# Eight column sums of a modulation product: reduced after a transpose, or by one-column matmuls

## The reference: what is computed

```python
def modulation(cond, ada_w, ada_b):
    mod = jax.nn.silu(cond) @ ada_w + ada_b            # ada_w: 2048 x 18432
    return jnp.split(mod[..., None, :], N_MOD, axis=-1)
...
sh1, sc1, g1, sh2, sc2, g2, sh3, sc3, g3 = modulation(c, ada_w[l], ada_b[l])
xs = ffn_sublayer(xs, sh1, sc1, g1, norm_ffn1_w[l], ffn1_wi[l], ffn1_wo[l])
mq, mk, mv, mo, mg, aq, ak, av, gm, ga = mixer_inputs(xs, sh2, sc2, norm_mix_w[l], w_in[l])
hm, _ = mlstm_branch(...)                              # 4 heads, two directions
ha = latent_attention(...)                             # 16 query heads, 4 key heads
xs = xs + g2 * merge_branches(hm, ha, gm, ga, w_proj_m[l], w_proj_a[l], w_out[l])
xs = ffn_sublayer(xs, sh3, sc3, g3, norm_ffn2_w[l], ffn2_wi[l], ffn2_wo[l])
```

## Time and profile before

| | |
|---|---|
| median of three runs | 2280.02 us |
| the profiled execution's own time | 2280.02 us |
| its span, first to last instruction | 2278.2 us |
| TensorE matmul busy | 2234.8 us (98%) in 10699 matmuls |
| VectorE busy | 1525.6 us (67%) |
| ScalarE busy | 934.5 us (41%) |
| TensorE's share of the chain that ended last | 93% |
| granted TensorE clock | 0.998 |

### The profile page before, as it was taken

How to read it: one execution, slowest core, us unless ns; L and a number is a source line. 1 busy time by engine, 2 the same in 40 slices (tenths; PEclk the granted TensorE clock), 3 DMA queues, 4 the chain that set the end, 5 groups by cost and what they waited for, 6 DMA issues and landing times.

```text
span 2278.2 us, 28667 instructions
## 1 busy us (share of the span) xinstructions
PE 2234.8 (98%) x10699; PEld 1773.9 (78%) x10699; DVE 1525.6 (67%) x1746; ACT 934.5 (41%) x1096; POOL 63.0 (3%) x54
## 2 busy tenths in 40 slices
PE   6999999999999998999999999999999999999998
PEld 3567777777777777888878888888888888888887
DVE  3445766677667768854866888656567676776757
ACT  3333333333333335544554444445444443444442
POOL 0010000000000000000500000100000000000000
PEclk9999999999999999999999999999999999999999
DMA  9998878878887875553635777646576757657563
GB/s 362 377 377 298 298 280 284 287 269 303 278 293 257 312 278 185 193 184 123 212 117 190 257 256 252 207 165 197 191 259 193 263 189 249 196 195 261 185 225 125
DMA packets 273216, 548.08 MB, mean 241 GB/s; under 512 B 9022, under 2 KB 9222, under 8 KB 272896
## 3 DMA queue, kind: packets, MB, share of 16 engines
q1 hardware_dynamic: 212388, 421.59, 54.5%
q10 hardware_dynamic: 57740, 115.90, 14.3%
q0 software_dynamic: 3024, 9.71, 1.4%
HBM read 543.71 MB, written 3.46 MB: 240 GB/s over the span
## 4 chain that ended last, share of the span: by engine, by line
PE 93%; DVE 4%; DMA 2%; issue 1%; ACT 1%; SPq 0%; POOL 0%; ACTq 0%; DVEq 0%; POOLq 0%
PE ps L663 29%; PE ps L665 28%; PE ps L664 28%; PE ps L576 3%; DMA ada_w_sb<-in_ada_w 1%; DVE w_lo L1654 1%; PE ps L747 1%; DMA gate_bc<-gate_dram 1%; PE ps L617 0%; PE ps L589 0%; PE ps L598 0%; PE ps L650 0%; PE ps L609 0%; PE ps L991 0%; PE ps L1059 0%
## 5 line engine op out<-in xcount | busy, mean ns | idle before, releaser
L1654 DVE TENSOR_TENSOR w_lo<-raw_w,w_hi 128x1024 fp32r<-128x1024 f32 x728 | 896.9, 1234 | 570.2 <-ACT w_hi L1233 567.9
L1233 ACT CAST w_hi<-raw_w 128x1024 fp32r<-128x1024 f32 x728 | 764.6, 1052 | 1190.6 <-PE ps L665 1138.7
L663 PE MATMUL ps<-w_hi,xT_hi 128*128 128x512 f32 x2080 | 823.4, 396 | 6.7 <-DVE xT_lo L1734 4.0
L665 PE MATMUL ps<-w_hi,xT_lo 128*128 128x512 f32 x2080 | 810.8, 390 | 0.0
L664 PE MATMUL ps<-w_lo,xT_hi 128*128 128x512 f32 x2080 | 810.2, 390 | 0.0
L663 PEld LDWEIGHTS ps<-w_hi,xT_hi 128*128 128x128 f32 x2080 | 390.7, 188 | 114.2 <-issue 26.8
L665 PEld LDWEIGHTS ps<-w_hi,xT_lo 128*128 128x128 f32 x2080 | 390.7, 188 | 82.7
L664 PEld LDWEIGHTS ps<-w_lo,xT_hi 128*128 128x128 f32 x2080 | 391.1, 188 | 78.2
L663 PE MATMUL ps<-w_hi,hT_hi 128*128 128x512 f32 x704 | 277.8, 395 | 5.6 <-DVE hT_lo L1803 2.8
L665 PE MATMUL ps<-w_hi,hT_lo 128*128 128x512 f32 x704 | 274.7, 390 | 0.0
L664 PE MATMUL ps<-w_lo,hT_hi 128*128 128x512 f32 x704 | 274.5, 390 | 0.0
(11 more groups left out here) (276 smaller groups left out, 1017.7 us busy)
## 6 DMA issues: line engine op xcount, KB each, us to landing
raw_w<-in_ffn_wi SPq DMA_DIRECT2D x176, 1024.0 KB, 5.2
ada_w_sb<-in_ada_w ACTq DMA_DIRECT2D x96, 1024.0 KB, 7.5
raw_w<-in_ffn_wo SPq DMA_DIRECT2D x88, 1024.0 KB, 5.1
raw_w<-in_w_in SPq DMA_DIRECT2D x68, 1024.0 KB, 5.3
ada_w_sb<-in_ada_w SPq DMA_DIRECT2D x30, 1024.0 KB, 12.7
raw_w<-in_w_out SPq DMA_DIRECT2D x16, 1024.0 KB, 5.2
ada_m<-in_ada_w ACTq DMA_DIRECT2D x12, 1024.0 KB, 5.6
raw_w<-in_w_proj_m SPq DMA_DIRECT2D x8, 1024.0 KB, 5.1
```

Of the source, the lines that this page charges most:

```text
L663: pe.matmul(out, a_hi, w_hi[:, slot, kk, :], start=(first and kk == 0), stop=False)
L665: mm = pe.matmul(out, a_lo, w_hi[:, slot, kk, :], start=False, stop=(last and kk == 1))
L1233: act.copy(w_hi[:, us % SPL, :, :], raw_w[:, slot, 2 * half:2 * half + 2, :]).then_inc(hi_ready, 1)
L1654: dve.tensor_tensor(w_lo[:, us % SPL, :, :], raw_w[:, slot, 2 * half:2 * half + 2, :], w_hi[:, us % SPL, :, :].bitcast(F32), ALU.subtract) ...
```

## The change

`vec_T` becomes `column_sums`. Each of the eight 128x128 blocks of an accumulator is now the stationary operand of a float32 matmul whose moving operand is one column of ones. The sum over partitions comes out in one column of PSUM, 8 columns for each accumulator, all in bank 6. `sum_cols` loses the reduction and adds the bias straight from PSUM. In `U_OUT` the three accumulators are summed at one place, after unit 9, and one addition on VectorE takes all three. In `U_IN` the sum moves from after unit 27 to after unit 24, and its addition from VectorE's step 28 to step 26. `MACS_Z` spreads the 32 MACs evenly over steps 2 to 22, two in even and one in odd steps.

```diff
-MACS_Z = macs_at(*((v, 1 if v in (5, 9, 13) else 2) for v in range(2, 17)), (22, 2), (23, 2), (25, 1))
+MACS_Z = macs_at(*((v, 2 if v % 2 == 0 else 1) for v in range(2, 23)), (23, 0))
...
-            def vec_T(c, vec, done, bank):
+            def column_sums(c, accs, done):
 
                 pe.wait_ge(ada_cols_done, c)
                 pe.wait_ge(mac_done, done)
-                for g in range(GROUPS):
+                for n, vec in enumerate(accs):
                     for b in range(4):
-                        mm = pe.transpose(ps[:, bank + g, b * P:(b + 1) * P], vec[:, g, b * P:(b + 1) * P], ident)
-                mm.then_inc(acc_T_done, 1)
+                        for g in range(GROUPS):
+                            at = 8 * n + 2 * b + g
+                            mm = pe.matmul(ps[:, 6, at:at + 1], vec[:, g, b * P:(b + 1) * P], ctile[:, 0, 16:17], start=True, stop=True)
+                mm.then_inc(ada_summed, len(accs))
...
-                                vec_T(t + 4 * G3 - 1, vec_acc, t * VEC + VEC_F2, 6)
+                                column_sums(t + 4 * G3 - 1, [vec_acc], t * VEC + VEC_F2)
...
-                if v == 11:
-                    vec_T(VCH, vec_acc, VEC_M, 6)
+                if v == 8:
+                    column_sums(VCH, [vec_acc], VEC_M)
...
                     if n == 1 and k == 1:
-                        vec_T(VCH + 1, vec_m[0], VEC_F2, 4)
-                        vec_T(VCH + 1, vec_m[1], VEC_F2, 6)
-                    if n == 2 and k == 1:
-                        vec_T(VCH + 3, vec_m[2], VEC_F2, 4)
+                        column_sums(VCH + 1, vec_m, VEC_F2)
...
-            def sum_cols(c, bank):
-
-                n = c - VCH + 1
-                dve.wait_ge(ada_cols_done, c)
-                dve.wait_ge(acc_T_done, n)
-                dve.tensor_reduce(small[:, 48:56], ps[:, bank:bank + 2, :].rearrange("p g (b k) -> p (g b) k", k=P), AX.X, ALU.add
-                                  ).then_inc(acc_summed, 1)
-                dve.wait_ge(acc_summed, n)
-                dve.tensor_tensor(adacols[:, bass.ds(4 * c, 4), :], small[:, 48:56].rearrange("p (g b) -> p b g", g=GROUPS),
-                                  biascol[:, bass.ds(4 * c - 4 * VCH, 4)].unsqueeze(2).to_broadcast([P, 4, GROUPS]),
-                                  ALU.add).then_inc(ada_cols_done, 1)
+            def sum_cols(c, many=1):
+                dve.wait_ge(ada_summed, c + many - VCH)
+                dve.tensor_tensor(adacols[:, bass.ds(4 * c, 4 * many), :],
+                                  ps[:, 6, 0:8 * many].rearrange("p (b g) -> p b g", g=GROUPS),
+                                  biascol[:, bass.ds(4 * c - 4 * VCH, 4 * many)].unsqueeze(2).to_broadcast([P, 4 * many, GROUPS]),
+                                  ALU.add).then_inc(ada_cols_done, many)
...
-                if v == 28:
-                    sum_cols(VCH, 6)
+                if v == 26:
+                    sum_cols(VCH)
...
-                    if n == 1 and k in (2, 3):
-                        sum_cols(VCH - 1 + k, 2 * k)
-                    if n == 2 and k == 2:
-                        sum_cols(VCH + 3, 4)
+                    if n == 1 and k == 4:
+                        sum_cols(VCH + 1, 3)
```

More of the change, by code:

```diff
@@ L281, in build @@
         ada_x_landed = sems("ada_x_landed", 2)
-        one_ready, mac_done, acc_T_done, acc_summed = sem("one_ready"), sem("mac_done"), sem("acc_T_done"), sem("acc_summed")
+        one_ready, mac_done, ada_summed = sem("one_ready"), sem("mac_done"), sem("ada_summed")
         ada_m_landed = sems("ada_m_landed", 2)
@@ L1849, in ffn_out @@
                             if v and k == 4:
-                                sum_cols(c, 6)
+                                sum_cols(c)
                         if k % 2:
```

## The result

The changed kernel took 2293.83 us (median of five runs, 2291.13 to 2295.98), the kernel before 2280.12 us (2279.12 to 2281.82). The ratio is 1.0058 with a 95% interval of 1.0044 to 1.0074. It is slower, as forecast, but by 13.7 us and not by 8.6. It lies outside the range of 2286.0 to 2291.0 us.

A forecast was written before the change was run, and what follows sets the result against it. TensorE, busy 98% of the span, was taken as the bound. Matmul pairs +7.2, the wait for `lf` +1.5 and the scan -0.1 gave +8.6 on 2280.0: 2288.6 us, range 2286.0 to 2291.0.

The forecast's parts named there:

- Part 1: At the eight sums, the removed transposes cost TensorE 0.885 us per accumulator, 7.1 us in all.
- part 2: At the eight sums, 16 pairs of 0.112 us cost 1.79 us each, +7.2 us net in all.
- Part 3: On VectorE, dropping eight 1.22 us reductions and two additions frees 9.7 us, costed at nothing.
- Part 4: In `U_IN` steps 17 to 20, moved MACs delay `lf` and TensorE waits 1.53 us; bounds 0 to 2.0.
- the scan gains 0.09 us: At the scan's transpose in `U_IN`, column sums standing ahead remove TensorE's wait for VectorE, -0.09 us.
- The three sums gathered in `U_OUT` are the same 24 calls as at two places, 3 x 0.90 of the 7.2: In `U_OUT`, gathering three sums at one place adds nothing beyond their 3 x 0.90 us share.
- D: At the sums, 16 loads in a row make pairs slower, 0.16 us each: 2294.9 us; chance 0.05.
- A: In `U_IN`, no wait for `lf` comes; matmuls cost as forecast: +7.1, 2287.1 us; chance 0.17.
- B: At the sums, one pair per call, so only the `lf` wait remains: +1.5, 2281.5 us; chance 0.07.
- C: At the sums, products run at their moving operand's pace: faster, 2272.9 us in the limit; chance 0.03.

The follow-up runs named there:

- both edits: Changed kernel with the gathered sums at three places in `U_OUT` and the previous `MACS_Z` and `U_IN` places restored; 2287.63 us.
- Three places: Changed kernel with the 24 gathered `U_OUT` products split, after units 9, 13 and 17; 2289.22 us.
- old table: Changed kernel with the previous `MACS_Z` and the previous `U_IN` places of sum and addition, gathered sums kept; 2292.75 us.
- the last version: Kernel before, but VectorE transposes 32x32 blocks and reduces; TensorE adds four partition groups with a 32-column stationary operand; 2276.02 us.

## Why the prediction was wrong

- *Part 1 and part 2, pairs of float32 products:* right. Two pairs for each call, 1.80 us a sum against 1.79, and the isolated cost of all eight +7.1 us (both edits) against 7.2.
- *Part 3, VectorE's saving at nothing:* right. Its busy time fell by 10 us, and the kernel with the pairs alone is still slower by the whole cost of the pairs.
- *Part 4, the wait for `lf`:* right in place, cause and size, 1.54 us by starts against 1.53. Only its price was not whole. In four of seven profiles a stretch of 3.4 us at the lower clock follows, 1.6 us more. That the scan gains 0.09 us was a misreading: the gap before its transpose stayed when the scan had long been ready.
- *"The three sums gathered in `U_OUT` are the same 24 calls as at two places, 3 x 0.90 of the 7.2":* this step failed. It priced gathering at nothing, and the whole prediction takes TensorE's clock as constant. In the profiled execution the gathered sums cost 2.7 us more for pairs, as forecast, and 4.9 us for the lower clock, 2.0 of which fall on the ordinary matmuls behind them. Three places take away 4.6 us of the time, and 128 moving columns at the same place keep the clock up.
- The rivals: D named slower pairs with 0.16 us; the average in `U_OUT` was 8.26 / 48 = 0.172, but by the clock and only there, and the single sums stay at 0.1125. Its mechanism is wrong though its time of 2294.9 us lies nearest. So its near hit is luck. A, B and C fell: the wait came, there are two records for each call, and a sum costs 1.80 us.
- The forecast's +8.6 us with the two clock costs of the profiled execution, 4.9 and 1.6, is 15.1 us. The medians show 13.7, and this execution got there by a first block that was 1.5 us early. In other executions the lower clock costs less: it lasts 3.4 to 10.2 us in `U_OUT` and comes four times in seven behind the wait.

What stays open: why the stretch in `U_OUT` differs so much between executions, and why the wait brings one only sometimes. Why one-column products bring the clock down and products of 128 columns do not is not shown either, nor where between 16 and 48 pairs, or between 1 and 128 columns, it begins. The old table's gain is not settled by time (1.1 us, 3.0 expected); between the traces it is 4.08 - 0.92 = 3.16 us.

## What to carry to other kernels

When TensorE is the bound and the moving operands are short, count its load-and-multiply pairs and not its columns: here a float32 product cost two pairs of 0.112 us with 1, 4 or 128 moving columns, while a float32 transpose cost one. And be wary of gathering products with very narrow moving operands. Spread between long matmuls, 16 pairs at a time, they cost only their pairs; 48 in a row (5.4 us) were followed by 3.4 to 10.2 us at half the clock. A stretch at the lower clock hides in a busy share of 100%, so look at the granted clock of the window. And where times scatter by more than the effect, compare the same piece of the program between two traces.

## What the runs showed of the hardware

- In the last version a float32 pair with a stationary operand of 32 columns and 8 moving ones cost 0.38 / 8 = 0.048 us, where pairs with 128 stationary columns cost 0.112. Its four products also write to four different groups of 32 partitions, and no run tells which of the two made the pairs cheaper.
- 16 one-column pairs in a row (1.8 us) left the clock up at every one of their places; 48 (5.4 us) brought it down in three profiles of three; 48 transposes (5.2 us) or 48 pairs of 128 columns (5.3 us) left it up.
- A wait of TensorE with 1.4 us of idle time was followed by 3.4 us at the lower clock in four profiles of seven. In the stage with waits of up to 2.5 to 3.0 us, 880 to 905 us, there were 3.4 or 6.8 us of it in twelve of twelve.
- Single stretches of 3.4 us at the lower clock come and go between executions near 65, 95 or 125 us, in the first feed-forward block, in seven profiles of twelve. By the cost of the others each is worth some 1.6 us; how much of the 3 to 6 us by which runs of one kernel differ is theirs is not shown.
